# Where VectorE takes a step's side work: before or after the low part of that step's half chunk

## The chip, the cores and the metric

The kernel runs on one core of a Trainium2 chip. Its time is the device time of one launch in microseconds (us); the median of three launches is given, and one more launch was profiled. The core's engines work through queues of their own, in order, and meet only through semaphores: TensorE (PE in the profile; PEld is its weight load), VectorE (DVE), ScalarE (ACT), GpSimd (POOL) and SyncE (SP), which issues most DMAs.

## What is computed

Four layers on 256 tokens of width 2048, in float32, one after another. Layer 1 (here the DSA layer) projects the tokens to 20480 columns, rotates queries and keys, attends in three windowed patterns over 16 heads, joins the three results by their log-sum-exps, gates and projects back. Layer 2 (MLA) is latent attention with low-rank projections. Both end in a residual sum and a layer norm. Layers 3 and 4 are alike: an RMS norm with shift and scale from a vector c, a projection to 7704 columns, three mixers side by side (gated linear attention, a gated delta rule with a short convolution, differential attention), and an output projection with a gate.

```python
h = x @ w_in                      # layer 1; then per group g of 3
o, l = dilated_window_attention(q, k, v, window, dilation)
o = einsum('gbsh,gbshd->bshd', softmax(stack(lses), 0), stack(outs))
y = (o * silu(z)) @ w_out
...
shift, scale, gate = split(silu(c) @ w_ada[l] + b_ada[l], 3)   # layers 3 and 4
h = (rms_norm_2(x, norm_w[l]) * (1 + scale) + shift) @ w_in[l]
x = x + gate * (concatenate([o_gla, o_gdn, o_diff]) @ w_out[l])
```

## The kernel before

Nearly all of the work is `X @ W` with weights that stream from memory once. Each float32 product is made of three fast ones: the weights are split into a high part (rounded, `w_hi`) and a low part (`w_lo = w_raw - w_hi`), the tokens likewise (`xt_hi`, `xt_lo`), and TensorE adds lo x hi, hi x lo and hi x hi.

The unit is a **half chunk**: two blocks of 128 rows by 512 columns of a weight. For each half chunk `h`

- SyncE loads the chunk (two halves, 1 MB) into one of four `w_raw` buffers once the low part of the half seven before is done (line 424), and in the first stage also the next pieces of `w_ada` (lines 427 to 433), each of which waits for the piece three before to be used;
- ScalarE rounds it, `round_half` (line 1067), once TensorE has finished half `h - 4`, since `w_hi` and `w_lo` hold four halves;
- VectorE makes the low part, `low_half` (line 1566), once ScalarE has rounded;
- TensorE multiplies, `half_chunk` (lines 505 to 507) or `half` (lines 1038 to 1040, and 1030 to 1033 for three blocks), 12 matmuls of 512 columns, once the low part is there.

Everything else is **side work**, cut into steps that carry a slot number. Each engine holds its own generator of steps (`windows` in the first stage, `mixers(l)` in the last two layers) and `side.upto(slot)` runs those that are due. TensorE runs the steps of slot `s` right after half `s`. ScalarE and VectorE run those of slot `s` in the step of half `h = s + 3`: ScalarE after `round_half(s + 3)` (lines 1175 to 1183), VectorE after `low_half(s + 3)` (lines 1831 to 1838 and 2567 to 2571). The order within each engine's queue is thus written out by hand.

**The first stage** has 320 halves of the DSA input projection and 32 of its output projection. Twelve attention groups run beside it. A group has ticks at six slots, two slots apart, from slot `B - 2` on (`TICKS`, `group_base`). In tick `k` TensorE makes the scores of head `k` (line 564, waits for the maxima of head `k - 1`), turns the probabilities of head `k - 1` (line 571, waits for ScalarE's exponentials) and attends for head `k - 2` (lines 579 to 581). VectorE's tick is `maxima` of head `k` (lines 1602 to 1614) and the update of head `k - 2` (lines 1706 to 1713). ScalarE's tick is the copy of the turned probabilities (line 1108) and the exponentials (lines 1100 to 1102). Besides the ticks VectorE has two steps that are not in `windows`: `dsa_evac`, the rotation of a finished block of queries or keys (lines 1591 to 1596, at slots 7 and 8 of a block), and `ada(slot)`, one piece of `c @ w_ada` in four dependent operations (line 1684), in most slots without a tick. At the stage's end `y_turns` makes the low parts of the turned attention result (line 1737).

**The last two layers** have 152 halves each after a seam that isn't touched. Their `mixers(l)` is a long chain over the three mixers in which TensorE, ScalarE and VectorE hand results to each other in nearly every slot: `level` of the gated delta rule (line 2295, with the semaphore increment at 2297) feeds TensorE's lines 848 and 853; `diff_scaled` (lines 2258 to 2264, with the rotation in lines 2078 to 2083) feeds line 956; `maxima` and `update` serve the ticks as in the first stage. The gated residual sums (`gated`) come behind `side.upto` and are not moved.

The MLA layer has the same loop (lines 1972 to 1983) and is not changed.

Of the kernel before, what the change touches and what calls it, by code (L numbers as in the profile page):

```python
# [97 lines left out]
def chunk_at(c0, h):  # L98

    return c0 + (h - NARROW) // 2  # L100
# [90 lines left out]
def program(nc, io, out):  # L191
    with ExitStack() as ctx:
# [88 lines left out]
        def S(name):  # L281

            if name not in named:
                named[name] = sem(name)
            return named[name]
# [1270 lines left out]
        def _(dve):  # L1556
# [5 lines left out]
            def low_half(c, q, n=BW):  # L1562

                ks = slice(2 * q, 2 * q + 2)
                dve.wait_ge(hi_made, 2 * c + q + 1)
                V.tensor_tensor(WL[:, c % 2, ks, 0:n], RAW[:, c % 4, ks, 0:n], WH[:, c % 2, ks, 0:n].bitcast(F32),  # L1566
                                ALU.subtract).then_inc(lo_made, 1)
# [101 lines left out]
            def ada(slot):  # L1669

                for a in ada_pieces(slot):
                    e, k0 = a // ADA_K, 2 * (a % ADA_K)
                    if k0 == 0 and e > 1:
                        dve.wait_ge(ada_columned, e - 1)
                    dve.wait_ge(ada_loaded[a % 3], 16 * (a // 3) + 16)
                    for k in range(2):
                        for half in range(2):
                            cols = slice(256 * half, 256 * half + 256)
                            o, w, c = ACC[:, e % 2, cols], ARAW[:, a % 3, k, cols], small[:, 48 + k0 + k:49 + k0 + k]
                            if k0 + k == 0:  # L1680
                                own(V.tensor_scalar(o, w, c, None, ALU.mult))
                            else:
                                dve.wait_ge(dve_self, own.n - 1)
                                own(V.scalar_tensor_tensor(out=o, in0=w, scalar=c, in1=o, op0=ALU.mult, op1=ALU.add))  # L1684
                    own.sync()
                    dve.sem_inc(ada_used, 1)
                    if k0 == 14:
                        dve.sem_inc(ada_summed, 1)
# [40 lines left out]
            def y_turns():  # L1729

                last = group_base(DSA_ITERS - 1, 2)
                for g in range(4):
                    for t in range(T):
                        yield last + (2 * g + t + 2 if g < 3 else 15)
                        dve.wait_ge(turn_hi, 8 + 2 * g + t + 1)
                        cols = slice(t * P, (t + 1) * P)
                        V.tensor_tensor(XTL[:, 4 * g:4 * g + 4, cols],
                                        TP[t if g == 3 else 1][:, :].rearrange("p (k s) -> p k s", k=4),
                                        XTH[:, 4 * g:4 * g + 4, cols].bitcast(F32), ALU.subtract).then_inc(turn_lo, 1)

            def dsa_evac(b, t):

                i, kind = b // DSA_BLOCKS, b % DSA_BLOCKS
                if kind < 9 and kind % 3 < 2:
                    g, qk = kind // 3, kind % 3
                    if t == 0:
                        block_done(4 * b + 3)
                        dve.wait_ge((q_turned, k_turned)[qk], 1 + i * 3 + g)
                    own.sync()
                    own(rotate((QN, KN)[qk][:, t, :].rearrange("p (h n) -> p h n", h=4),  # L1750
                               PJ[b % 2][t][:, :].rearrange("p (h n) -> p h n", h=4), ROPE_A[:, t], 4, 64, TMP))
                    own.sync()
                    dve.sem_inc(roped, 1)
                if t == 1:
                    dve.sem_inc(dve_evacuated, 1)
# [72 lines left out]

            side, turns = Side(windows()), Side(y_turns())
            for h in range(DSA_HALVES + 32):  # L1830
                low_half(h // 2, h % 2)
                slot = h - 3
                if slot >= 7 and slot % 8 in (7, 0) and slot <= DSA_HALVES:
                    dsa_evac((slot - 7) // 8, (slot + 1) % 8)
                side.upto(slot)
                turns.upto(slot)
                if slot >= 0:
                    ada(slot)
                if slot == DSA_HALVES + 16:
                    dve.wait_ge(ada_columned, DEPTH * ADA_COLS)  # L1840
                    dve.wait_ge(S("ada_rows"), 1)
                    own(V.tensor_tensor(ADC[:, 0:96], ADC[:, 0:96], SP[:, 384:480], ALU.add))
                    own.sync()
                    for l in range(LAYERS):
                        sc = ADC[:, 48 * l + 16:48 * l + 32]
                        own(V.scalar_tensor_tensor(out=sc, in0=sc, scalar=1.0, in1=ADC[:, 96 + 16 * l:112 + 16 * l],
                                                   op0=ALU.add, op1=ALU.mult))
                    own.sync()
                if slot >= DSA_HALVES and slot % 2 and (slot - DSA_HALVES) // 2 in OUT_LAST:
                    b = OUT_LAST.index((slot - DSA_HALVES) // 2)  # L1850
                    out_block(C_DSA_OUT, B_DSA_OUT + b, b)
# [118 lines left out]
            side, turns = Side(heads()), Side(mla_turns())  # L1970
            dve.sem_inc(dve_evacuated, 2)
            for h in range(FULL + 1, MLA_HALVES + 32):
# [5 lines left out]
                slot = h - 3  # L1978
# [561 lines left out]
            for l in range(LAYERS):  # L2540
                c0, b0 = C_LAYERS + l * LAYER_CHUNKS, B_LAYERS + l * LAYER_BLOCKS
                out0 = chunk_at(c0, IN_HALVES)

                def gated(t, b):

                    cols = slice(b * BW, (b + 1) * BW)
                    o = SQD[:, t * BW:(t + 1) * BW]
                    own(V.tensor_tensor(o, PJ[(b0 + b) % 2][t][:, :], GT[:, cols], ALU.mult))
                    own.sync()
                    if t == 1:  # L2550
                        dve.sem_inc(dve_evacuated, 1)
                    own(V.tensor_tensor(X[:, t, cols], X[:, t, cols], o, ALU.add))

                def gated_last(t):

                    if t == 0:
                        dve.wait_ge(S("first_tokens"), 2 + l + 1)
                    else:
                        block_done(out0 + OUT_LAST[3])
                    gated(t, 3)  # L2560
                    own.sync()
                    dve.sem_inc(S("x_block"), 1)

                side = Side(mixers(l))
                dve.sem_inc(dve_evacuated, 2)
                for h in range(FULL + 1, HALVES):
                    low_half(chunk_at(c0, h), h % 2)
                    if h < IN_HALVES and h % 8 == 0:
                        dve.sem_inc(dve_evacuated, 1)
                    slot = h - 3  # L2570
                    side.upto(slot)
                    if slot == CLEAR_AT and l + 1 < LAYERS:
                        clear()
                    if slot >= IN_HALVES and slot % 2 and (slot - IN_HALVES) // 2 in OUT_LAST:
                        b = OUT_LAST.index((slot - IN_HALVES) // 2)
                        block_done(out0 + OUT_LAST[b])
                        own.sync()
                        for t in range(T):
                            gated(t, b)
                        own.sync()  # L2580
                        dve.sem_inc(S("x_block"), 1)
                if l + 1 < LAYERS:
                    c1 = c0 + LAYER_CHUNKS
                    gated_last(0)
                    low_narrow(c1, IN_COLS[0][1])
                    rms_arg(0, 8 + 7)
                    rms_take(0)
                    affine(l + 1, 0)
                    gated_last(1)
                    lo_h(l + 1, 0)  # L2590
                    rms_arg(1, 8 + 8)
                    affine(l + 1, 1)
                    rms_take(1)
                    lo_h(l + 1, 1)
                    affine(l + 1, 2)
                    lo_h(l + 1, 2)
                    affine(l + 1, 3)
                    lo_h(l + 1, 3)
                    low_half(chunk_at(c1, FULL), 0)
                    for i in range(4, 8):  # L2600
                        affine(l + 1, i)
                        lo_h(l + 1, i)
                else:
                    for t in range(T):
                        gated_last(t)
# [76 lines left out]
```

## Time and profile before

| | us |
|---|---|
| median of three launches (2704.64 to 2707.52) | 2706.74 |
| the profiled launch | 2705.5 |
| its span, first to last instruction | 2703.7 |
| busy: TensorE matmul / weight load | 2599.2 / 2196.7 |
| busy: VectorE / ScalarE | 1987.5 / 1204.3 |

The span is what the rows divide up; 1.8 us of the profiled launch lie outside it. Times of rows are microseconds from the span's start. Matmuls are pipelined: a row's duration is longer than its distance to the next row, so distances between starts tell more of TensorE than its busy share does. A row of a timeline may stand for several instructions (x4); what stands in brackets is the engine's idle time before it and what ended it. The DSA input projection lies at 34 to 1063 us, the MLA layer at about 1175 to 1565, the two last layers at 1643 to 2104 and 2211 to 2671 between their seams.

### The profile page before, as it was taken

To read this page: it belongs to the slowest core of one execution; us is meant where nothing else is said; L and a number is where in the kernel's file an instruction comes from. 1 tells how busy PE (TensorE), PEld (TensorE's weight loads), DVE (VectorE), ACT (ScalarE), POOL (GpSimd) and SP (SyncE) were. 2 spreads that over 40 slices of the span, in tenths; PEclk is the share of its full clock that TensorE was granted. 3 is DMA by queue.
4 is the path that set the end of the run, shared out by engine and by line. 5 is a ranking of instruction groups with operands and counts; after the bars stand their busy time and mean duration, and the time that the engine had idled before them with its cause. 6 is when DMAs were issued, how large, how long until landed. Compare 5 with 4: busy or idle time off the path is not lost.

```text
span 2703.7 us, 34528 instructions
## 1 busy us (share of the span) xinstructions
PE 2599.2 (96%) x13199; PEld 2196.7 (81%) x13199; DVE 1987.5 (74%) x3385; ACT 1204.3 (45%) x1747; POOL 15.1 (1%) x32
## 2 busy tenths in 40 slices
PE   5999999999999999999999979999999999999999
PEld 4888788878888887888888779878788898888887
DVE  6888888898889887556555666667887567568875
ACT  3443444444443444335555345443445354433453
POOL 0000000000000000000000000000000000000000
PEclk9999999999999999979999969999999899999999
DMA  7777777777687776535444525434445354434444
GB/s 262 280 265 258 247 255 281 260 264 269 235 277 280 247 263 227 186 125 177 143 133 172 175 75 172 140 125 130 135 156 169 113 168 146 139 125 140 136 160 140
DMA packets 265045, 517.03 MB, mean 191 GB/s; under 512 B 16496, under 2 KB 20784, under 8 KB 263984
## 3 DMA queue, kind: packets, MB, share of 16 engines
q1 hardware_dynamic: 263280, 508.43, 55.3%
q0 software_dynamic: 1600, 6.38, 0.9%
q8 instruction: 105, 1.72, 0.3%
q14 instruction: 60, 0.49, 0.1%
HBM read 512.68 MB, written 2.10 MB: 190 GB/s over the span
## 4 chain that ended last, share of the span: by engine, by line
PE 56%; DVE 25%; issue 11%; ACT 6%; DMA 1%; DVEq 0%; SPq 0%; ACTq 0%
DVE arena L1684 8%; PE proj L505 7%; PE proj L507 7%; PE proj L506 7%; PE proj L1038 5%; PE proj L1039 5%; PE proj L1040 5%; DVE w_lo L1566 4%; ACT w_hi L1067 2%; PE proj L1030 2%; PE proj L1033 2%; PE proj L1032 2%; PE scores L564 1%; DVE arena L1602 1%; ACT arena L1102 1%
## 5 line engine op out<-in xcount | busy, mean ns | idle before, releaser
L1566 DVE TENSOR_TENSOR w_lo<-w_raw,w_hi 128x1024 fp32r<-128x1024 f32 (+1 forms) x768 | 932.5, 1219 | 482.8 <-ACT w_hi L1067 425.7
L1067 ACT ACTIVATE w_hi<-w_raw 128x1024 fp32r<-128x1024 f32 (+1 forms) x768 | 802.2, 1052 | 716.0 <-PE proj L507 397.4
L505 PE MATMUL proj<-w_hi,xt_lo 128*128 128x512 f32 x1696 | 679.6, 401 | 4.3 <-DVE w_lo L1566 4.3
L507 PE MATMUL proj<-w_hi,xt_hi 128*128 128x512 f32 x1696 | 664.5, 392 | 0.0
L506 PE MATMUL proj<-w_lo,xt_hi 128*128 128x512 f32 x1696 | 664.1, 392 | 0.0
L1038 PE MATMUL proj<-w_hi,xt_lo 128*128 128x512 f32 x992 | 402.5, 406 | 0.0
L1040 PE MATMUL proj<-w_hi,xt_hi 128*128 128x512 f32 x992 | 387.8, 391 | 0.0
L1039 PE MATMUL proj<-w_lo,xt_hi 128*128 128x512 f32 x992 | 387.6, 391 | 0.0
L505 PEld LDWEIGHTS proj<-w_hi,xt_lo 128*128 128x128 f32 x1696 | 320.8, 189 | 74.4 <-DVE w_lo L1566 6.8
L507 PEld LDWEIGHTS proj<-w_hi,xt_hi 128*128 128x128 f32 x1696 | 320.3, 189 | 68.8
L506 PEld LDWEIGHTS proj<-w_lo,xt_hi 128*128 128x128 f32 x1696 | 321.0, 189 | 62.6
L1684 DVE SCALAR_TENSOR_TENSOR arena<-arena,small 128x256 f32<-128x256 f32 x720 | 301.0, 478 | 0.8 <-DVE y L1725 0.8
L1040 PEld LDWEIGHTS proj<-w_hi,xt_hi 128*128 128x128 f32 x992 | 186.7, 188 | 40.0
L1039 PEld LDWEIGHTS proj<-w_lo,xt_hi 128*128 128x128 f32 x992 | 187.4, 189 | 34.8
L1038 PEld LDWEIGHTS proj<-w_hi,xt_lo 128*128 128x128 f32 x992 | 187.3, 189 | 34.7
L1030 PE MATMUL proj<-xt_lo,w_hi 128*128 128x256 f32 x384 | 112.0, 292 | 0.0
L1032 PE MATMUL proj<-xt_hi,w_lo 128*128 128x256 f32 x384 | 110.3, 287 | 0.0
L1033 PE MATMUL proj<-xt_hi,w_hi 128*128 128x256 f32 x384 | 110.3, 287 | 0.0
L1101 ACT ACTIVATE arena<-arena 128x128 f32<-128x128 f32 x80 | 31.7, 396 | 155.6 <-DVE arena L1610 155.6
L564 PE MATMUL scores<-arena 128*128 128x256 f32 (+3 forms) x384 | 86.7, 343 | 3.5 <-DVE arena L1610 2.4
L564 PEld LDWEIGHTS scores<-arena 128*128 128x128 f32 (+1 forms) x384 | 57.2, 189 | 23.9 <-issue 5.3
L1030 PEld LDWEIGHTS proj<-xt_lo,w_hi 128*128 128x128 f32 x384 | 75.7, 197 | 0.1
(352 smaller groups left out, 2785.7 us busy)
## 6 DMA issues: line engine op xcount, KB each, us to landing
w_raw<-in_dsa_w_in_dram SPq DMA_DIRECT2D x160, 1024.0 KB, 7.5
w_raw<-in_w_in_dram SPq DMA_DIRECT2D x120, 1024.0 KB, 5.0
arena<-in_w_ada_dram SPq DMA_DIRECT2D x192, 512.0 KB, 5.8
w_raw<-in_w_out_dram SPq DMA_DIRECT2D x32, 1024.0 KB, 5.0
w_raw<-in_mla_w_in_dram SPq DMA_DIRECT2D x24, 1024.0 KB, 5.1
w_raw<-in_dsa_w_out_dram SPq DMA_DIRECT2D x16, 1024.0 KB, 5.0
w_raw<-in_mla_w_out_dram SPq DMA_DIRECT2D x16, 1024.0 KB, 5.1
w_raw<-in_mla_w_ukv_dram SPq DMA_DIRECT2D x8, 1024.0 KB, 5.2
```

The lines of the kernel that those rows point to most:

```text
L505: mm(o, xt[1][:, k0 + kk, tok], WH[:, c % 2, k, 0:n], start=first, stop=False)
L506: mm(o, xt[0][:, k0 + kk, tok], WL[:, c % 2, k, 0:n], start=False, stop=False)
L507: ins = mm(o, xt[0][:, k0 + kk, tok], WH[:, c % 2, k, 0:n], start=False, stop=last)
L564: ins = mm(o, q[:, t * P:(t + 1) * P], kk[:, 0:(t + 1) * P], start=a == 0, stop=a == len(parts) - 1)
L1030: mm(o, WH[:, w, k, f], XTL[:, kk, :], start=first and ct % 2 == 0, stop=False, skip_group_check=True)
L1032: mm(o, WL[:, w, k, f], XTH[:, kk, :], start=False, stop=False, skip_group_check=True)
L1038: mm(o, XTL[:, kk, tok], WH[:, w, k, :], start=first, stop=False)
L1039: mm(o, XTH[:, kk, tok], WL[:, w, k, :], start=False, stop=False)
L1040: ins = mm(o, XTH[:, kk, tok], WH[:, w, k, :], start=False, stop=last)
L1067: A(WH[:, c % 2, 2 * q:2 * q + 2, 0:n], RAW[:, c % 4, 2 * q:2 * q + 2, 0:n], ACT.Copy).then_inc(hi_made, 1)
L1566: V.tensor_tensor(WL[:, c % 2, ks, 0:n], RAW[:, c % 4, ks, 0:n], WH[:, c % 2, ks, 0:n].bitcast(F32), ALU.subtract).then_inc(lo_made, 1)
L1684: own(V.scalar_tensor_tensor(out=o, in0=w, scalar=c, in1=o, op0=ALU.mult, op1=ALU.add))
```

## The change

In the loop of the first stage and in that of the last two layers VectorE runs `side.upto(slot)` ahead of `low_half` of half `slot + 3`, instead of behind it. In the first stage the evacuation `dsa_evac`, `turns.upto` and `ada` keep their places behind the low part, so side work now also stands ahead of `dsa_evac`. In the last layers the increment of `dve_evacuated` and all that followed `side.upto` keep theirs. No instruction is added, removed or resized, no semaphore or wait count is altered, and the other engines' queues are the same.

```diff
@@ the first stage (VectorE)
             for h in range(DSA_HALVES + 32):
+                slot = h - 3
+                side.upto(slot)
                 low_half(h // 2, h % 2)
-                slot = h - 3
                 if slot >= 7 and slot % 8 in (7, 0) and slot <= DSA_HALVES:
                     dsa_evac((slot - 7) // 8, (slot + 1) % 8)
-                side.upto(slot)
                 turns.upto(slot)
                 if slot >= 0:
                     ada(slot)
@@ the last two layers (VectorE)
                 for h in range(FULL + 1, HALVES):
+                    slot = h - 3
+                    side.upto(slot)
                     low_half(chunk_at(c0, h), h % 2)
                     if h < IN_HALVES and h % 8 == 0:
                         dve.sem_inc(dve_evacuated, 1)
-                    slot = h - 3
-                    side.upto(slot)
                     if slot == CLEAR_AT and l + 1 < LAYERS:
                         clear()
```

## Rows read from the trace of the kernel before

**Rows 1.** Page, busy time and share of the span by engine.

```profile
PE 2599.2 (96%) x13199; PEld 2196.7 (81%) x13199; DVE 1987.5 (74%) x3385; ACT 1204.3 (45%) x1747; POOL 15.1 (1%) x32
```

**Rows 2.** Windows: stretch, its length, busy PE, PEld, DVE, ACT, POOL, clock, DMA, GB/s.

```profile
34.00:1063.00 1029.00, 1008.99 (x4818) 831.78 (x4819) 886.45 (x1656) 445.52 (x679) 0.00 (x0) 0.99 0.74 261
```

**Rows 3.** Waits, 34 to 1063 us: who for whom, us in total, times, longest.

```profile
PE turn L655 <- DVE xt_lo L1737: 4.7, 1, 4.7
...
PEld turn L571 <- ACT arena L1102: 20.3, 28, 1.6
PEld proj L505 <- DVE w_lo L1566: 6.8, 15, 0.9
...
PEld scores L564 <- DVE arena L1614: 4.9, 10, 1.1
PEld scores L564 <- DVE arena L1610: 3.5, 5, 1.3
...
DVE w_lo L1566 <- ACT w_hi L1067: 89.4, 55, 2.5
```

**Rows 4.** Chain of waits, 520 to 545 us: start, us, what (longest pieces).

```profile
529.63 1.68 DVE arena L1684 x4
...
532.59 0.56 DVE arena L1602
...
535.29 0.96 ACT w_hi L1067
...
537.41 1.68 DVE arena L1684 x4
```

**Rows 5.** Timelines of DVE, PE and PEld, 523 to 537 us.

```profile
523.67 1.23 DVE L1566 TENSOR_TENSOR w_lo<-w_raw,w_hi 128x1024 fp32r<-128x1024 f32 x1
...
528.54 0.48 PE L505 MATMUL proj<-w_hi,xt_lo 128*128 128x512 f32 x1
...
533.85 0.39 PE L507 MATMUL proj<-w_hi,xt_hi 128*128 128x512 f32 x1
...
536.32 0.48 PE L505 MATMUL proj<-w_hi,xt_lo 128*128 128x512 f32 x1
...
534.23 0.52 PEld L564 LDWEIGHTS scores<-arena 128*128 128x128 f32 x4 [0.42 <-DVE arena L1614]
535.34 0.31 PEld L571 LDWEIGHTS turn<-constants,arena 128*128 128x128 f32 x3 [0.59 <-ACT arena L1102]
```

**Rows 6.** Timeline of PE, a tick that waits for nothing.

```profile
448.52 0.39 PE L507 MATMUL proj<-w_hi,xt_hi 128*128 128x512 f32 x1
...
450.32 0.47 PE L505 MATMUL proj<-w_hi,xt_lo 128*128 128x512 f32 x1
```

**Rows 7.** Waits of PE, 2211 to 2671 us.

```profile
PE turn L848 <- DVEq L2297: 3.9, 2, 2.0
PE turn L956 <- DVEq L2264: 1.9, 2, 1.6
PE turn L853 <- DVEq L2297: 1.9, 1, 1.9
...
PE turn L571 <- ACT arena L1108: 1.5, 4, 0.6
```

**Rows 8.** Timelines of DVE, at three places of the last layer, and of PE.

```profile
2268.99 1.23 DVE L1566 TENSOR_TENSOR w_lo<-w_raw,w_hi 128x1024 fp32r<-128x1024 f32 x1 [2.45 <-ACT w_hi L1067]
...
2492.99 1.23 DVE L1566 TENSOR_TENSOR w_lo<-w_raw,w_hi 128x1024 fp32r<-128x1024 f32 x1 [1.29 <-ACT w_hi L1067]
...
2560.74 1.22 DVE L1566 TENSOR_TENSOR w_lo<-w_raw,w_hi 128x1024 fp32r<-128x1024 f32 x1
...
2563.63 2.37 DVE L1566 TENSOR_TENSOR w_lo<-w_raw,w_hi 128x1024 fp32r<-128x1024 f32 x2
...
2563.04 0.39 PE L1038 MATMUL proj<-w_hi,xt_lo 128*128 128x512 f32 x1
```

**Rows 9.** Windows: 5 us around a half at the lower clock, columns as in rows 2.

```profile
209.00:214.00 5.00, 5.00 (x17) 4.03 (x17) 4.67 (x11) 1.69 (x3) 0.00 (x0) 0.66 0.65 200
```

## The prediction

> **What bounds the kernel now.** I read the page first. TensorE is busy for 96% of the span, VectorE for 74% [rows 1], so the engine whose queue is reordered is not the one that sets the end. A reordering can only pay where TensorE waits for something that VectorE delivers late. By stretches, the first stage is the one where VectorE has little to spare: 886 us busy of 1029 [rows 2]. The waits of that stage then show two things. VectorE itself sits idle for 89.4 us in 55 places, all waiting for a rounded half chunk of ScalarE. And TensorE's weight loads sit idle in the ticks, 28 times for exponentials (20.3 us) and 15 times for maxima (4.9 and 3.5 us) [rows 3]. An engine that is idle while its consumer waits is stuck in a loop, and the chain of waits shows the loop: at 529.63 `ada`, at 532.59 the maxima, at 535.29 ScalarE's rounding, at 537.41 `ada` again [rows 4]. That is 7.78 us for two slots. In this loop are `ada` (1.82, to the low part behind it), a low part (1.14), maxima and exponentials together (535.29 - 532.59 = 2.7, of them 1.6 the maxima), a rounding (1.0) and **a second low part** (1.14, as from 536.31 to the next `ada`); they add up to 7.8. The exponentials hold up the next rounding, the rounding the next low part, and the low part stands ahead of the next maxima, although the scores were there.
>
> What it costs TensorE is read from the starts of products. A tick that waits for nothing has 1.80 us from its last product before to its first after [rows 6]; the tick of the loop has 536.32 - 533.85 = 2.47 [rows 5], so 0.67 are lost. The weight loads of this tick show 0.42 + 0.59 = 1.01 of idle time [rows 5]: they count 0.34 too much for each tick. So the 28.7 us of the stage are 28.7 - 28 x 0.34 = 19.2 us of lost TensorE time.
>
> **The change part by part, first stage.** Nothing is added. The tick (maxima and update) changes places with one low part.
>
> The loop. With the maxima ahead of the low part, the way from one maxima to the next is: maxima 1.6, exponentials 1.0, rounding 1.07, low part 1.14, `ada` 1.82, together 6.6 us. VectorE's own work in the two slots is 2 x 1.14 + 1.82 + 1.6 + 0.9 (update) = 6.6. TensorE needs 7.78 - 0.67 = 7.1 for its two halves and the tick. All three numbers are now below or at TensorE's, so the loop stops binding and TensorE sets the pace. I take the whole 19.2 us. Bounds: 0 if the loop only changes its shape, 28.7 if the idle time of the weight loads counts in full.
>
> The end of the stage. TensorE waits 4.7 us once for the low part of a turned result (line 1737) [rows 3], made by `turns.upto`, which stays behind the low part. VectorE comes to it late because it idled in the ticks before, in the loop above (89.4 / 55 = 1.6 us a time [rows 3]). With those gone I keep 1.2 us of the wait: VectorE still has to do a tick (2.5), a low part (1.14) and to wait for ScalarE's copy within TensorE's next half (2.7). Gain 3.5, bounds 0 and 4.7.
>
> What is late next. Where slots with `ada` follow each other, VectorE needs 2.96 us for a slot (1.14 + 1.82) and TensorE 2.72, and TensorE waits there for low parts: 6.8 us in 15 places [rows 3]. The change takes no work from VectorE, so this stays, and part of the gain is given back there. VectorE enters such a stretch earlier by the idle time that it is spared, so I take only 2.0 us more, between 0 and another 6.8.
>
> Moved past. `side.upto` now also stands ahead of `dsa_evac` in the two slots of a window that are evacuation slots. The rotated block is turned three or four slots later, and its buffer is needed eight slots later, so 2.5 us are covered by at least two halves (5.4). If that cover were gone, it would be one tick for each window. SyncE's loads wait for the low part of the half seven before the one that they bring; a tick of 2.5 us fits into the slots between, three of them at least, while a load waits for `ada` pieces in any case, which keep their place. POOL waits for nothing here. Cost nothing.
>
> First stage: -19.2 - 3.5 + 2.0 = -20.7 us.
>
> **The last two layers.** In one layer TensorE waits 3.9 us for `level` (L848), 1.9 us for it at the next step (L853), 1.9 for the rotated queries and keys (L956) and 1.5 in the ticks [rows 7]. A side step comes earlier by the change only if VectorE was idle at a low part before it; if VectorE waited inside a side step, as many low parts as before stand ahead of the next ones. At `level` it was idle for 2.45 us two steps before, at the rotation for 1.29 [rows 8], to which there the low part of 1.14 comes. Both are above the longest single waits, 2.0 and 1.6 [rows 7]. So L848 goes (-3.9), of L956 the 1.6 go, the tick waits go (-1.5), and L853 stays, as its producer waits for TensorE's step before.
>
> Against it: a low part is now late by the side step ahead of it. Its lead over its product is mostly above 4 us here. At the tightest place it ends at 2561.96 and its product starts at 2563.04, a lead of 1.08, and the side step that moves ahead of it takes from 2561.88 to 2563.55, 1.7 us [rows 8]. That costs 0.6, and the low part before it, with a longer step, about as much: +1.1 together. Bounds: 0, and 3 if the gains before it take the lead away.
>
> One layer: -3.9 - 1.6 - 1.5 + 1.1 = -5.9; both alike, -11.8 us.
>
> **Sum.** -20.7 - 11.8 = -32.5. The profiled span was 2703.7, so 2671.2; with the 1.8 us outside it 2673.0, and the median of the runs lies 1.2 above the profiled launch: **2674**.
>
> A word on TensorE's clock. Between 209 and 214 us the granted clock was 0.66 [rows 9], that is, part of it at 1.2 GHz: 5 x 0.34 = 1.7 us lost, right after a tick. The Trainium skill (TensorE: Matmul & The Clock Gate, "What's actually happening") says that TensorE falls to half rate after idleness and comes back after sustained work. By that rule fewer waits would also spare this, and the sum would be lower by up to some 5 us if the stage has three such places; by the row alone, which shows it once in 5 us and not in every tick, I leave it out of the sum and in the range.
>
> **Rivals.**
> - *VectorE binds the first stage.* For: 2.96 us against 2.72 where `ada` is dense, and TensorE already waits for low parts there. What the ticks gain is then lost before the next window. Against: outside its 89.4 us of waiting VectorE has some 939 us of work in a stage that TensorE needs about 1000 for. Then only the layers gain: 2706.7 - 11.8 = 2695. Chance 0.13.
> - *The low parts come too late (slower).* Mechanism: in a tick VectorE now waits for TensorE's scores before it makes the low part of a half three later. The low part at 523.67 ends at 524.90 and its product starts at 528.54, a lead of 3.6 us [rows 5]; with a tick of 2.5 ahead of it 1.1 are left. It decides from the point where VectorE reaches the tick later than 1.1 us after the scores. If each of the 48 full ticks (12 windows of 4) then loses 0.5 us and gains nothing, that is +24, and with the layers' -11.8 +12: 2719. For: windows that VectorE enters late exist. Against: a late VectorE has its maxima earlier than before in any order, and the pair's work (6.6) is below TensorE's (7.1), so it catches up. The Trainium skill (TensorE: Matmul & The Clock Gate, "Architectural detail: the array is 16x 32x32, not 1x 128x128") says that VectorE's queue is strictly first in, first out; by that rule everything behind a waiting tick waits with it, which is this rival. Chance 0.08.
> - *It does nothing in effect.* The exponentials, not the maxima, set the ticks, and ScalarE is late for reasons of its own. Against: ScalarE is busy for only 445 of 1029 us [rows 2]. Then 2707. Chance 0.03.
>
> **How the numbers follow.** My forecast has 0.76. Its own range goes from 2656 (tick idle time in full, 4.7 in full, no more waits for low parts, the clock) to 2688 (half of the first stage's gain). A measurement of this kernel tells about 0.2% from no change, 5.4 us. Faster by more than that: the forecast and the first rival, less a little for a smaller gain than either, 0.87; within it 0.04; slower 0.09. The range takes in the first rival and leaves the slower one out: 2656 to 2700.
>
> **What would show it.** Right: in a window of the first stage the maxima start right after the scores, two slots take about 7.1 us instead of 7.78, ScalarE's waits for maxima and VectorE's for `w_hi` shrink, the wait at line 655 falls to about 1, the stage ends about 20 us earlier; in the layers the wait of line 848 is gone and that of line 853 stays. Wrong: TensorE's waits for `w_lo` grow from 6.8 to 20 us or more, above all right after ticks, or the stage's length stays while the waits only change their names.

## The result and the profile after

The kernel after takes **2665.67 us** (median of 5 runs, 2665.41 to 2667.07), the kernel before 2707.12 beside it (2704.64 to 2708.21). The ratio is 0.9849, with a 95% interval from 0.9836 to 0.9863: 1.5% faster. The forecast was 2674, in a range of 2656 to 2700. The profiled span fell from 2703.7 to 2665.3, by 38.4 us; the medians differ by 41.4, as the profiled launch of after is the longest of its five and that of before lies 1.6 below its median.

Two rows of the page of the kernel before (shares of the chain that ended last; the low parts), and then the page of the kernel after, whose first row is to be read against [rows 1]:

```profile
PE 56%; DVE 25%; issue 11%; ACT 6%; DMA 1%; DVEq 0%; SPq 0%; ACTq 0%
...
L1566 DVE TENSOR_TENSOR w_lo<-w_raw,w_hi 128x1024 fp32r<-128x1024 f32 (+1 forms) x768 | 932.5, 1219 | 482.8 <-ACT w_hi L1067 425.7
```

```profile
PE 2585.1 (97%) x13199; PEld 2199.4 (83%) x13199; DVE 1988.8 (75%) x3385; ACT 1209.4 (45%) x1747; POOL 15.1 (1%) x32
...
PE 82%; DVE 13%; issue 3%; ACT 1%; DMA 0%; DVEq 0%; SPq 0%; ACTq 0%
...
L1566 DVE TENSOR_TENSOR w_lo<-w_raw,w_hi 128x1024 fp32r<-128x1024 f32 (+1 forms) x768 | 929.3, 1218 | 323.9 <-ACT w_hi L1067 264.2
```

The same instructions, with the same durations. What changed is who stands on the chain that ended last: before, TensorE held 56% of it, VectorE 25% and ScalarE 6%; now TensorE holds 82%. VectorE's idle time ahead of the low parts fell from 482.8 to 323.9 us, in an engine that has as much work as before.

Windows of the kernel after, the same 1029 us as in [rows 2] (the stage now ends some 26 us earlier, so the row holds a little of the next one):

```profile
34.00:1063.00 1029.00, 1023.27 (x4950) 857.38 (x4951) 903.98 (x1680) 463.51 (x695) 1.20 (x2) 0.99 0.75 267
```

Waits of the kernel after in its first stage, 34 to 1036 us, against [rows 3]:

```profile
ACT arena L1100 <- DVE arena L1614: 80.3, 32, 6.2
...
DVE w_lo L1566 <- ACT w_hi L1067: 33.3, 42, 3.4
...
DVE arena L1602 <- DVE arena L1684: 9.7, 38, 0.6
...
DVE arena L1602 <- PE scores L564: 6.3, 6, 4.2
...
PE turn L655 <- DVE xt_lo L1737: 3.9, 2, 3.5
...
PE proj L505 <- DVE w_lo L1566: 3.2, 2, 2.7
...
PEld proj L505 <- DVE w_lo L1566: 1.8, 3, 0.9
...
PEld turn L571 <- ACT arena L1102: 0.4, 1, 0.4
```

The weight loads' wait for the exponentials went from 20.3 us in 28 places to 0.4 in one; the waits for the maxima (L1614, L1610) are no longer in the list; VectorE's wait for rounded half chunks went from 89.4 to 33.3. The waits for low parts at line 505 did not grow: the matmuls' went from 4.3 to 3.2, the weight loads' from 6.8 to 1.8. The wait at line 655 is still there, with 3.5 us in its longest place.

Timelines of the kernel after, DVE and then PE, over the two slots that [rows 4, 5] show of before:

```profile
519.72 0.56 DVE L1602 SCALAR_TENSOR_TENSOR arena<-scores,constants 128x384 f32<-128x384 f32 x1 [0.22 <-DVE arena L1684]
...
521.15 0.16 DVE L1614 TENSOR_TENSOR arena<-arena 128x2 f32<-128x2 f32 x1
521.23 0.60 DVE L1709 SCALAR_TENSOR_TENSOR arena<-arena,attended 128x128 f32<-128x128 f32 x2
...
522.24 2.40 DVE L1566 TENSOR_TENSOR w_lo<-w_raw,w_hi 128x1024 fp32r<-128x1024 f32 x2
524.56 1.66 DVE L1684 SCALAR_TENSOR_TENSOR arena<-arena,small 128x256 f32<-128x256 f32 x4
526.44 0.56 DVE L1602 SCALAR_TENSOR_TENSOR arena<-scores,constants 128x384 f32<-128x384 f32 x1 [0.22 <-DVE arena L1684]
...
517.58 0.82 PE L564 MATMUL scores<-arena 128*128 128x128 f32 x4
...
519.15 0.47 PE L505 MATMUL proj<-w_hi,xt_lo 128*128 128x512 f32 x1
...
526.27 0.47 PE L505 MATMUL proj<-w_hi,xt_lo 128*128 128x512 f32 x1
```

The maxima follow `ada` with 0.22 us of idle time, and both low parts come in one piece behind the update, without a wait. From maxima to maxima VectorE takes 526.44 - 519.72 = 6.72 us, and TensorE 526.27 - 519.15 = 7.12 for the same two halves that took it 536.32 - 528.54 = 7.78 in [rows 5]. The forecast was 6.6 and 7.1. One sign came otherwise: the maxima were to start right after the scores. They start 1.3 us after these end (517.58 + 0.82 = 518.40, and 519.72), since `ada` stands ahead of them, and so it is in 38 places; in 6 they wait for scores.

Where the 38.4 us are, by the starts of the first product of each half chunk in the two traces: from the first half to half 320 of the first stage 1035.8 became 1009.6, that is 26.2 of them (3.4, 7.6, 9.2 and 6.0 in the four groups of 80 halves); from there to the first product of layer 3 the kernel after is 0.4 longer; from first to last half but one, layer 3 520.5 to 513.1 (7.4) and layer 4 517.4 to 512.6 (4.8).

### The profile page after: what moved, and what is told of

It reads as the page before. It is cut to its first block, busy times and chain, and to the rows that moved or that the text cites. A ratio compares the mean times of both kernels' runs of the same rounds, so it can differ in the third digit from the quotient of the medians.

```text
span 2665.3 us, 34528 instructions
## 1 busy us (share of the span) xinstructions
PE 2585.1 (97%) x13199; PEld 2199.4 (83%) x13199; DVE 1988.8 (75%) x3385; ACT 1209.4 (45%) x1747; POOL 15.1 (1%) x32
## 4 chain that ended last, share of the span: by engine, by line
PE 82%; DVE 13%; issue 3%; ACT 1%; DMA 0%; DVEq 0%; SPq 0%; ACTq 0%
PE proj L505 14%; PE proj L507 14%; PE proj L506 14%; PE proj L1038 7%; PE proj L1040 7%; PE proj L1039 6%; PE scores L564 3%; DVE w_lo L1566 2%; DVE arena L1684 2%; PE proj L1030 2%; PE proj L1033 2%; PE proj L1032 2%; PE turn L571 1%; PE attended L579 1%; PE attended L581 1%
## 5 line engine op out<-in xcount | busy, mean ns | idle before, releaser
L1566 DVE TENSOR_TENSOR w_lo<-w_raw,w_hi 128x1024 fp32r<-128x1024 f32 (+1 forms) x768 | 929.3, 1218 | 323.9 <-ACT w_hi L1067 264.2
L1602 DVE SCALAR_TENSOR_TENSOR arena<-scores,constants 128x384 f32<-128x384 f32 x80 | 44.5, 557 | 51.3 <-PE scores L564 41.4
```

## The experiments

Eleven kernels ran. Those of one group shared the runs of the kernel before, whose median was 2706.3 to 2706.5 in all three groups.

**1 and 2. Each half of the change alone.** The first hunk of the diff without the second, and the second without the first.

```
e1:  first stage    side.upto(slot)  ahead of  low_half(h // 2, h % 2)
e2:  late layers    side.upto(slot)  ahead of  low_half(chunk_at(c0, h), h % 2)
```

> Only the first stage has the new order. My theory (the loop through exponentials, rounding and low part is broken there): the whole gain of that stage and none elsewhere. By the product starts of the two traces the stage is 26.3 us shorter, so about 26 below the kernel before, 2681, with the late layers as long as before. Rival (the stage's gain needs nothing of its own, it came from another clock or from the layers): less than 15 below, above 2692.

> Only the last two layers have the new order. By the product starts they are 7.4 and 4.8 us shorter, one of them perhaps with 1.7 us of clock in it, so my theory gives 10 to 12 below the kernel before, 2695 to 2697; the wait of line 848 gone, that of line 853 there, and waits for the low part at line 1038. Prediction's figure for them: 11.8. Rival (the layers' gain is the clock, which follows from the shorter first stage): within 5 of the kernel before.

Measured: e1 2677.96 (28.3 below the kernel before; ratio 0.9898, 0.9883 to 0.9913), e2 2693.39 (12.9 below; 0.9955, 0.9940 to 0.9969). e1 gained 2 more than expected, e2 1 more. Together 41.2, and both at once gave 41.4: the parts add up, and the layers' gain is not borrowed from the first stage. By e2's product starts its layers are 7.7 and 4.9 us shorter.

**3 and 4. A load on the ring.** The reduction of line 1607 is made twice in every full tick of the first stage, once in the order of before and once in that of after.

```diff
                 own(V.tensor_reduce(MX[:, h, 1:2], SM[:, par, 128:384], AX_X, ALU.max))
+                if mask < 3:
+                    own.sync()
+                    own(V.tensor_reduce(MX[:, h, 1:2], SM[:, par, 128:384], AX_X, ALU.max))
```

> The order of before, with the 0.41 us reduction of line 1607 done twice in each of the 48 full ticks of the first stage (0.41 us more VectorE work and 0.41 later exponentials a tick; 19.7 us more work in all). Loop theory: the loop of 7.78 us for two slots has the maxima in it and TensorE waits in it, so each of the ticks that stall (28 of 48 by the rows) passes it on in full, and more of them stall: 28 x 0.41 = 11.5 up to 48 x 0.41 = 19.7 us slower than the kernel before. Rival (the exponentials set nothing, VectorE has its time): under 5 us slower.

> The order of after with the same second reduction. Loop theory: the loop is 6.6 + 0.41 = 7.0 and VectorE's work for the two slots also 7.0, against TensorE's 7.1, so nearly nothing passes through in the ticks: 0 to 6 us slower than the kernel after, and the distance between the two orders grows from 41 to 50 or more. Rival (VectorE's total work sets the stage in either order, and the change freed it): as much slower as the loaded kernel of before, 11 to 20.

Measured: e3 2729.61, 23.3 slower than the kernel before (1.0087, 1.0071 to 1.0104), more than the 19.7 expected at most; e4 2668.64, only 3.0 slower than the kernel after, with the same extra work, as expected. Timeline of the kernel before, DVE, one row, and then of e3, DVE, one turn of the ring:

```profile
536.27 1.23 DVE L1566 TENSOR_TENSOR w_lo<-w_raw,w_hi 128x1024 fp32r<-128x1024 f32 x1 [1.31 <-ACT w_hi L1067]
```

```profile
546.60 1.22 DVE L1566 TENSOR_TENSOR w_lo<-w_raw,w_hi 128x1024 fp32r<-128x1024 f32 x1 [1.31 <-ACT w_hi L1067]
547.74 1.67 DVE L1687 SCALAR_TENSOR_TENSOR arena<-arena,small 128x256 f32<-128x256 f32 x4
549.56 1.23 DVE L1566 TENSOR_TENSOR w_lo<-w_raw,w_hi 128x1024 fp32r<-128x1024 f32 x1
550.70 0.55 DVE L1602 SCALAR_TENSOR_TENSOR arena<-scores,constants 128x384 f32<-128x384 f32 x1
...
551.93 0.42 DVE L1610 TENSOR_REDUCE arena<-arena 128x1 f32<-128x256 f32 x1
...
554.84 1.23 DVE L1566 TENSOR_TENSOR w_lo<-w_raw,w_hi 128x1024 fp32r<-128x1024 f32 x1 [1.31 <-ACT w_hi L1067]
```

The turn is 554.84 - 546.60 = 8.24 us long, 7.78 and the extra 0.42 with its step between, and the wait for `w_hi` in it has the 1.31 us that it has in the kernel before: everything between the waits is in the ring, so here the load passes through whole. It does not in all ticks. By the product starts TensorE's gaps (the distance from the last product of a half to the first of the next, less the 0.23 us between products) grew in 30 of the 72 slots with ticks, mostly by 0.4 to 0.5 us, as one load, or by 0.8 to 0.9, as two, and hardly in the others; in all slots with ticks by 19.5 us, which is the top of what was expected. The rest of the 24.1 by which the stage is longer was not in that sum: 3.1 are two more half chunks at the lower clock (111 and 191, see below). Under the new order the load falls into slack. This sets the loop theory apart from the rival that VectorE's work binds: it would have made e4 as much slower as e3. In e4 the gaps of all slots with ticks grew by 1.5 us. VectorE has 923.12 us of work in e4's first 1029:

```profile
34.00:1063.00 1029.00, 1019.42 (x4934) 852.12 (x4935) 923.12 (x1726) 459.50 (x695) 1.20 (x2) 1.00 0.75 266
```

What e4 does lose is at other places. Waits of e4, 34 to 1063 us:

```profile
PE turn L655 <- DVE xt_lo L1740: 5.4, 2, 4.6
...
PEld proj L505 <- DVE w_lo L1566: 4.5, 7, 1.2
PE proj L505 <- DVE w_lo L1566: 4.5, 5, 2.7
```

The slack of the ticks is used up, VectorE comes later to the dense slots and to the turned results, and there the three rows are 1.5, 2.7 and 1.3 us longer than in the kernel after (the last two show partly the same waits, at the weight loads and at the products). Half 316 was 1.1 us shorter there, which hides a part.

**5 and 10. Which part of the tick matters.** A second call of `side.upto` behind the low part, and one `yield` in `windows` that puts either the update (e5) or the maxima (e10) behind it. e5 stands on the kernel after, e10 on the kernel before with `side.upto(slot)` moved ahead of the low part as well.

```diff
                 side.upto(slot)
                 low_half(h // 2, h % 2)
+                side.upto(slot + 0.5)
...
e5:                          if k >= 2:
+                                yield B + TICKS + 2 * k + 0.5
e10 (update ahead of the maxima in the code):
                             if k < 4:
+                                yield B + TICKS + 2 * k + 0.5
```

> The kernel after, but in the first stage only the maxima of a tick go ahead of the low part; the update of the running sums (0.9 us) stays behind it, as in the kernel before. Loop theory: the way exponentials to next maxima is what counts, and the update is not in it (it follows the maxima and only delays the low part), so this keeps the whole gain of the stage: within 3 us of the kernel after, a little below it where the 3.2 us of waits for low parts at line 505 shrink. Rival (the update was late as well, and TensorE's next products of the attended block wait for its buffer to be read): 5 to 20 above the kernel after, with new waits at line 579.

> The kernel before, with the opposite half of the change in the first stage: the update of the running sums and all other side steps go ahead of the low part, the maxima alone stay behind it. Loop theory: exponentials, rounding, low part, maxima are in a ring as before, so nothing of the stage's 28 us comes: within 5 of the kernel before. Rival (what helps is that any side work is done early, or that the attended block's buffer comes free earlier): 10 to 28 below it.

Measured: e5 2662.09 (0.9836, 0.9821 to 0.9850), 3.6 below the kernel after, a little more than the 3 expected. e10 2733.40 (1.0097, 1.0082 to 1.0112), 26.9 slower than the kernel before. That is a miss, outside what either theory had said of e10: "within 5" took the update to be outside the ring. In the order of before it is outside: it runs after the maxima, while ScalarE makes the exponentials. Put ahead of the low part, it is in the ring as well. Timeline of e10, DVE:

```profile
549.00 1.23 DVE L1566 TENSOR_TENSOR w_lo<-w_raw,w_hi 128x1024 fp32r<-128x1024 f32 x1
550.14 0.55 DVE L1602 SCALAR_TENSOR_TENSOR arena<-scores,constants 128x384 f32<-128x384 f32 x1
...
551.57 0.16 DVE L1614 TENSOR_TENSOR arena<-arena 128x2 f32<-128x2 f32 x1
553.83 1.22 DVE L1566 TENSOR_TENSOR w_lo<-w_raw,w_hi 128x1024 fp32r<-128x1024 f32 x1 [2.10 <-ACT w_hi L1067]
554.97 1.67 DVE L1684 SCALAR_TENSOR_TENSOR arena<-arena,small 128x256 f32<-128x256 f32 x4
556.88 0.61 DVE L1706 SCALAR_TENSOR_TENSOR arena<-arena,attended 128x128 f32<-128x128 f32 x2 [0.24 <-DVE arena L1684]
...
557.90 2.36 DVE L1566 TENSOR_TENSOR w_lo<-w_raw,w_hi 128x1024 fp32r<-128x1024 f32 x2
```

VectorE now idles for 2.10 us while the exponentials and the rounding run, with no update to fill it (the kernel before idles for 1.31), and then does the update (556.88 to 557.90, 1.0 us) with the maxima waiting behind it. The two halves there take 9.17 us (545.08 to 554.25 by the first products) in place of 7.78. By the product starts the gaps in the slots with ticks grew by 18.0 us, those at slots 67 and 317 by 4.6. Its waits look like those of e3 (34 to 1063 us):

```profile
PEld turn L571 <- ACT arena L1102: 31.0, 32, 2.6
...
PEld scores L564 <- DVE arena L1614: 11.9, 12, 1.5
```

So "do side work early" is not what helps. With the maxima ahead of the low part the stage has its gain, with them behind it has none; the update moved in front, with the maxima left behind, costs as much as that gives (the other side steps of the stage, moved with it, have no share that these runs separate); behind the maxima but ahead of the low part, as in the kernel after, it costs a few us. By e5's product starts the ticks gain nothing by its removal (82.8 and 82.5 us of gaps); what is gained lies elsewhere: 0.6 us at slot 67, where TensorE (L590) waits for a semaphore of VectorE (L1688) in the kernel after, and at the turned results. Waits of e5 in the first stage:

```profile
PE turn L655 <- DVE xt_lo L1738: 2.8, 2, 2.4
```

**6. The turned results ahead as well.**

```diff
                 side.upto(slot)
+                turns.upto(slot)
                 low_half(h // 2, h % 2)
...
-                turns.upto(slot)
```

> The kernel after, with the turned results' low parts of the first stage (the wait of line 655, 3.5 us at slot 315) ahead of the low part of the half chunk as well. If VectorE reaches them late because of the low part ahead of them (1.2 us), the wait falls to about 2.3 and the time by 1.2; the prediction's reason (VectorE comes late because of the ticks' idle time) is wrong in any case, since 3.5 are left with that time gone. If ScalarE's copy or TensorE's own turn sets them, no change: within 0.5 of the kernel after.

Measured: 2667.03 (2662.4 to 2668.3; 0.9851, 0.9836 to 0.9866): no difference that these runs tell, and the two expectations (1.2 less, or within 0.5) are too near each other for them. Waits of e6 in the first stage:

```profile
PE turn L655 <- DVE xt_lo L1737: 3.1, 1, 3.1
```

Only 0.4 us of 3.5 go. The low part of line 1737 itself now waits 0.84 us for ScalarE's copy (L1152). That copy stands in ScalarE's queue behind the exponentials, which wait for the maxima of that slot. With the update behind the low part (e5) VectorE comes to these maxima sooner, and TensorE's wait is 2.4.

**7. The old order in the tight slots of the late layers.**

```diff
+                    late = 106 <= slot <= 118 or slot == 128
+                    if not late:
+                        side.upto(slot)
                     low_half(chunk_at(c0, h), h % 2)
...
+                    if late:
+                        side.upto(slot)
```

> The kernel after, with the old order in the slots 106 to 118 and 128 of the late layers, where its product starts show 3.5 us lost in a layer to late low parts (line 1038 waits for w_lo, 5.8 us in PE and weight loads). If the losses are the side step ahead of the low part, two layers give back up to 7: 3 to 7 below the kernel after. If the losses are a debt from the slots before (VectorE has no more slack to give), nothing or the old waits come back: within 2.

Measured: 2660.95 (0.9831, 0.9817 to 0.9846), 4.7 below the kernel after and in the expected 3 to 7, but not for the reason given alone. By the product starts the two layers account for only 2.1 of it (first to last, 1079.0 us in the kernel after, 1076.9 here): the waits ahead of the halves 110, 111 and 131 (0.63, 0.49 and 0.91 in layer 3) are gone, and at 114 the gap grows from 1.93 to 2.36. The rest is in the first stage, whose code is the same: 1006.6 us to half 320 here, 1009.6 in the kernel after, 1007.8 in its second profile (e9). Half 316 took 2.86, 5.01 and 4.43 us in the three. Why it differs stays open.

**8. The same exchange in the layer between.**

```diff
+                slot = h - 3
+                side.upto(slot)
                 low_half(chunk_at(C_MLA_IN, h), h % 2, n)
...
-                slot = h - 3
-                side.upto(slot)
```

> The kernel after, with the same exchange in the layer between (the one stretch that kept its order). The loop is of the same kind there: a tick's maxima behind a low part. If it stalls there too, 3 to 10 below the kernel after; if its ticks have room (VectorE has no ada pieces there and is less busy), within 2.

Measured: 2669.86 (2666.9 to 2670.8; 0.9861, 0.9844 to 0.9877), 4.2 above the kernel after. A miss, on the other side from both expectations. Timelines of e8, DVE and PE:

```profile
1189.89 0.17 DVE L1777 TENSOR_SCALAR small<-small 128x16 f32<-128x16 f32 x1 [5.88 <-ACTq L1208]
...
1194.34 0.50 PE L505 MATMUL proj<-w_hi,xt_lo 128*128 128x512 f32 x1 [1.80 <-DVE w_lo L1566]
...
1219.10 0.50 PE L505 MATMUL proj<-w_hi,xt_lo 128*128 128x512 f32 x1 [1.80 <-DVE w_lo L1566]
```

Two new waits for low parts, 3.6 us, nearly the whole loss. At both places VectorE stands idle for 5.88 us at a side step that waits for ScalarE (L1208) and makes the low parts only behind it; in the kernel after one more low part is made ahead of that step, and the wait there is 3.10 us. This is the mechanism of the prediction's slower rival, though the waiting step is not a tick, in a stage where nothing stalled in the ticks that could have been gained.

**9 and 11. The kernel after again, and what helped together.** e11 has e5's split, e6's line, and the old order in the slots 106, 107, 108 and 128 of the late layers alone.

```diff
                 side.upto(slot)
+                turns.upto(slot)
                 low_half(h // 2, h % 2)
+                side.upto(slot + 0.5)
...
+                    late = slot in (106, 107, 108, 128)
```

> The kernel after once more, so that the others of this group have it beside them: 2664 to 2668, 41 below the kernel before. If the differences of 3 to 5 between it and its variants are chance of the chip, it comes out at 2662 or lower.

> All that helped: in the first stage only maxima and the turned results' low parts go ahead of the low part, the update stays behind it; in the late layers the old order in the four slots 106, 107, 108 and 128. If the gains of the two earlier kernels (3.6 and 4.7 below the kernel after) are separate, 2657 to 2660; if most of the second was a difference in the clock of one half chunk (1.5 to 3 us at the end of the first stage), 2660 to 2662.

Measured: e9 2665.68 (2665.3 to 2666.1), as the kernel after had in another group, so the differences of 3 to 5 us between variants are not chance between groups. e11 **2658.19** (2656.5 to 2659.4; 0.9822, 0.9808 to 0.9837), 7.5 below the kernel after, in the range for separate gains, and 48.3 below the kernel before. Waits of e11, 34 to 1063 us:

```profile
DVE xt_lo L1738 <- ACT xt_hi L1152: 11.6, 5, 4.2
...
PE turn L655 <- DVE xt_lo L1738: 2.0, 1, 2.0
```

The wait of line 655 falls to 2.0. For the turned results VectorE now waits up to 4.2 us for ScalarE's copy, 1.6 us ahead of the one that TensorE waits for. By e11's product starts the first stage is 1003.3 us to half 320, layer 3 510.2 and layer 4 511.5.

## Why the prediction was right, and where it was off

**What bounds the kernel: right.** The ring of exponentials, rounding, low part and maxima was there, and the change opened it. Shown by e3 against e4 (23.3 and 3.0 us for the same load), and by e5 against e10 (the maxima ahead of the low part and the update behind it keep the gain; the other way about it is lost). In the kernel after, eight of the twelve groups have the very same gaps in their six ticks (0.46, 0.90, 1.57, 1.57, 1.82 and 0.58 us), and 1.57 is what the tick in [rows 6] shows that waits for nothing (1.80 less 0.23).

**Terms of the first stage** (forecast -20.7, measured -26.2 by the product starts):

- Ticks: forecast -19.2 (28.7 of idle weight loads less 28 x 0.34). The gaps between halves in the slots with ticks add up to 103.5 us before and 82.7 after: -20.8. The correction by 0.34 for each tick was needed; the full 28.7 would have been 8 too many.
- The wait at line 655: forecast -3.5, measured -1.2 (4.7 to 3.5). The step that failed was "VectorE comes to it late because it idled in the ticks before", with 1.2 us left for what stays. The idle time ahead of the low part before it fell from 2.09 to 0.96 us, and 3.5 were left. What holds it is the way of this slot's maxima, exponentials, copy (ScalarE) and low part (VectorE), with the update, `ada` and low parts of the half chunks in between: e6 takes 0.4, e5 1.1, both in e11 1.5. What sets the last 2.0 was not separated.
- Low parts in dense `ada` slots: forecast +2.0, a loss. This is the one step with the wrong sign. The slots without a side step have gaps of 8.8 us before and 5.8 after, of which 1.2 are line 655, so 1.8 were gained. The reason given, that VectorE has no less work and so must lose there, overlooked that it enters these slots with more lead: it is idle less (33.3 us of waiting for `w_hi` in place of 89.4) and as much work is done sooner. The text had this as the reason to take 2.0 and not 6.8; it went further. Two slots with side steps did lose, 0.6 us at slot 67 (see e5) and 0.4 at slot 317.
- The clock: left out of the sum, "up to some 5 us" in the range. Halves 55 and 215 took 4.41 and 4.43 us before and 2.85 each after: -3.1. The windows around both, before and then after (before: granted clock 0.66, as in [rows 9]; after: 1.00, so 2.4 GHz throughout):

```profile
724.00:729.00 5.00, 5.00 (x19) 4.09 (x20) 4.67 (x11) 1.93 (x3) 0.00 (x0) 0.66 0.38 142
```

```profile
207.00:212.00 5.00, 5.00 (x25) 4.18 (x25) 4.51 (x9) 1.45 (x2) 0.00 (x0) 1.00 1.04 381
706.50:711.50 5.00, 5.00 (x29) 4.26 (x28) 4.36 (x9) 2.00 (x2) 0.00 (x0) 1.00 0.77 265
```

  The rule of the Trainium skill (TensorE: Matmul & The Clock Gate, "What's actually happening"), by which fewer waits spare such stretches, agrees with this: e3, with more waits, has four such halves ahead of half 316 (4.41 to 4.52 us each), the kernel before two, the kernel after none. e2, which leaves the first stage alone, still has one at half 55.

These four terms give 20.8 + 1.2 + 1.8 + 3.1 = 26.9 against 26.2; half 316, which took 3.82 us before and 5.01 after, and the 1.0 of slots 67 and 317 are in the remainder, with smaller gains against them. So the sum was 5.5 too small: the clock (3.1), the low parts (3.8 from loss to gain) and the ticks (1.6) gave more than forecast, line 655 gave less (2.3).

**Terms of the late layers** (forecast -5.9 each, -11.8; measured -7.4 and -4.8, -12.2). The sum is right, its two sides were both too small. Waits of the kernel after in layer 4, 2178 to 2632 us, against [rows 7]:

```profile
PEld proj L1038 <- DVE w_lo L1566: 3.9, 5, 1.2
...
PE turn L853 <- DVEq L2297: 2.0, 1, 2.0
PE proj L1038 <- DVE w_lo L1566: 1.9, 3, 0.9
...
PE turn L956 <- DVEq L2264: 0.4, 1, 0.4
```

The wait of line 848 is gone and that of line 853 stays, as forecast; of L956 1.5 of 1.9 went. By gaps, the slots that gained give 8.4 us in layer 4 (forecast 7.0), and the halves 109 to 111, 114 to 116, 130 and 131 lose 3.0 (3.4 in layer 3; forecast 1.1, bound 3). The step that failed is the one that priced the low parts by two tight places in a row; the gaps grew at four slots, 109, 110, 114 and 130; e7 and e11 get back those of the halves 110, 111 and 131. Of the 2.6 us that layer 3 gained more than layer 4, 1.5 are its half 67, which took 4.37 us before and 2.83 after.

**The rivals.** That VectorE binds the first stage falls with e4. That low parts come too late (slower) did not decide in the first stage. The point from which it decides was named as 1.1 us of lateness behind the scores. That was too low: in the window shown above the maxima start 1.3 us behind them, and the low part behind the tick still ends some 2.8 us ahead of its product (522.24 + 1.2 = 523.44, and 526.27). The mechanism is real: e8 shows it twice with 1.80 us, and the late layers pay for it. The Trainium skill's rule that VectorE's queue is strictly first in, first out (the same page, "Architectural detail: the array is 16x 32x32, not 1x 128x128") agrees with e8 and with e10: in both, work that waits for nothing stands behind a waiting step.

Two smaller slips of the text: 939 us as VectorE's work is the stretch less one wait, and its busy time there is 886 [rows 2]; and half of the first stage's 20.7 with the layers' 11.8 gives 2685, not 2688, as the upper end of the forecast's own range. Nothing of the outcome hangs on either.

## What to carry to other kernels

Where two engines wait for each other while neither is full, write down the ring with its durations and look for an item that stands in it for no other reason than its place in an in-order queue; the gain is the ring less what the bounding engine needs (7.78 - 7.12 here), and not the idle time. Test such a ring with a small load: where the ring binds it passes through whole, in slack it vanishes. Move only the instruction that closes the ring, and only where it stalls: the rest of the same step cost 3.6 us, the same exchange in a stage without stalls 4.2.

## What was not expected of the hardware

The lower clock comes after stalls, but not after each. A half chunk of about 4.4 us in place of 2.85 turned up at the same half (55) in the kernel before, in e2 and in e3; e10 had such halves, 4.0 to 4.4 us long, at 68, 159 and 215; and between the first half chunk and half 316 none came in the kernels whose ticks don't stall, e4 among them. Each stood right behind a slot with a long gap between its products, 3.1 to 5.5 us. Yet of the four gaps of more than 3 us that the kernel before has ahead of slot 315 (3.23 at slot 54, 3.11 at 214, 3.20 at 238, 3.31 at 314) only the first two were followed by one, and e2 has the gap of 3.12 at slot 214 without it. At half 316, right after the wait of line 655, one came in every profiled kernel but e7, 3.8 to 5.1 us long. What decides whether one comes, and what sets its length, was not found.
